# One core, two transformer-like blocks: the first input tile loaded ahead of the constants, gate loads in four buffers, and the last products of a feed-forward layer in another order

## The reference, cut to what matters

```python
def first_block(x, ...):
    h = rms_norm(x, norm_mix_g[l])                    # x * rsqrt(mean(x*x) + eps) * g
    proj = h @ w_in[l]
    mla_cols, rw_cols, gate_cols = _split(proj, [MLA_COLS, RWKV_COLS, GATE_COLS])
    o_a = mla_branch(mla_cols, ...)                   # attention, 8 heads
    o_b = rwkv7_branch(rw_cols, ...)                  # a scan forward and one backward, norm, bonus, gate
    y_a = o_a @ w_o_l[:MLA_WIDTH]
    y_b = o_b @ w_o_l[MLA_WIDTH:]
    gates = jax.nn.sigmoid(gate_cols.reshape(B, S, N_BRANCHES, D) + b_gate[l])
    x = x + (gates[:, :, 0] * y_a + gates[:, :, 1] * y_b) @ w_merge[l]
    h = rms_norm(x, norm_ffn_g[l])
    gp = dwconv_centered(h @ w_ffn_gate[l], ffn_conv_w[l], ffn_conv_b[l])
    x = x + (jax.nn.silu(gp) * (h @ w_ffn_up[l])) @ w_ffn_down[l]
    return x

def second_block(x, ...):
    h = rmsnorm(x, norm1_g[l])
    ...                                               # gated linear attention and a convolution
    x = x + mixed
    h2 = rmsnorm(x, norm2_g[l])
    x = x + (jax.nn.silu(h2 @ w_ffn_gate[l]) * (h2 @ w_ffn_up[l])) @ w_ffn_down[l]
    return rmsnorm(x, norm_f_g)
```

## Time and profile before

| | |
|---|---|
| median of three runs | 3564.58 us (3561.55 to 3566.70) |
| the profiled execution, its own time | 3568.21 us |
| its span in the profile | 3566.4 us |
| PE busy | 3411.8 us, 96% |
| DVE busy | 1707.6 us, 48% |
| ACT busy | 1107.4 us, 31% |
| DMA | 269.82 MB, mean 76 GB/s |

### The profile page before, as it was taken

How to read it: one execution, slowest core, us unless ns; L and a number is a source line. 1 busy time by engine, 2 the same in 40 slices (tenths; PEclk the granted TensorE clock), 3 DMA queues, 4 the chain that set the end, 5 groups by cost and what they waited for, 6 DMA issues and landing times.

```text
span 3566.4 us, 60997 instructions
## 1 busy us (share of the span) xinstructions
PE 3411.8 (96%) x27176; PEld 2715.3 (76%) x27176; DVE 1707.6 (48%) x2528; ACT 1107.4 (31%) x1797; POOL 323.9 (9%) x342
## 2 busy tenths in 40 slices
PE   8989999999999998999999999899899999999998
PEld 7678776777777884578888888687677788888877
DVE  4353555666565566553345433542454522352236
ACT  4323324444444330132224212432332311241124
POOL 1232241111111212000000000001000000000000
PEclk9999999999999999999999999999899999999999
DMA  3241252111111304421112211222003111121122
GB/s 138 68 146 48 77 190 89 59 42 48 58 59 47 100 10 157 145 77 48 48 53 95 71 48 54 95 103 96 24 30 107 65 53 48 59 95 59 48 66 106
DMA packets 89974, 269.82 MB, mean 76 GB/s; under 512 B 11552, under 2 KB 12080, under 8 KB 89712
## 3 DMA queue, kind: packets, MB, share of 16 engines
q1 hardware_dynamic: 78960, 230.26, 19.6%
q0 software_dynamic: 10752, 35.66, 2.9%
HBM read 219.73 MB, written 46.14 MB: 75 GB/s over the span
## 4 chain that ended last, share of the span: by engine, by line
PE 85%; DVE 9%; ACT 3%; issue 2%; DMA 1%; POOL 0%; SPq 0%; DVEq 0%; ACTq 0%; POOLq 0%
PE ps L355 80%; PE ps L354 3%; PE ps L358 2%; DVE SM L375 2%; DVE AR L364 1%; DVE X L364 1%; ACT HT L1144 1%; DVE HT L368 1%; DVE W L364 1%; ACT WS L361 0%; DVE HL L364 0%; ACT W L2056 0%; DVE EX L364 0%; DMA qk_d<-AR 0%; DVE OTB L364 0%
## 5 line engine op out<-in xcount | busy, mean ns | idle before, releaser
L355 PE MATMUL ps<-HH,WS 128*128 128x512 f32 (+1 forms) x3232 | 1001.9, 391 | 0.0
L355 PEld LDWEIGHTS ps<-HH,WS 128*128 128x128 f32 (+1 forms) x3232 | 608.1, 188 | 129.9
L355 PE MATMUL ps<-HL,WS 128*128 128x512 f32 x1616 | 639.9, 396 | 7.1 <-DVE HL L364 6.9
L364 DVE TENSOR_TENSOR WS<-W,WS 128x1024 fp32r<-128x1024 f32 x244 | 298.4, 1223 | 638.2 <-ACT WS L361 638.2
L361 ACT ACTIVATE WS<-W 128x1024 fp32r<-128x1024 f32 x244 | 256.6, 1052 | 892.6 <-PE ps L355 885.4
L355 PE MATMUL ps<-WS,SA 128*128 128x512 f32 x2112 | 491.5, 395 | 23.3 <-DVE SA L364 21.0
L355 PEld LDWEIGHTS ps<-WS,SA 128*128 128x128 f32 x2112 | 401.3, 191 | 110.8 <-issue 27.2
L355 PEld LDWEIGHTS ps<-HL,WS 128*128 128x128 f32 x1616 | 304.1, 188 | 72.9 <-issue 7.4
L355 PE MATMUL ps<-HL,HI 128*128 128x512 f32 (+1 forms) x512 | 208.7, 408 | 4.3 <-POOL WL L364 2.8
L355 PE MATMUL ps<-AR 64*64 64x64 f32 (+2 forms) x4928 | 202.3, 241 | 10.0 <-ACT AR L361 4.2
L355 PE MATMUL ps<-WS,HH 128*128 128x512 f32 x640 | 204.4, 396 | 7.1 <-DVE HL L364 5.4
(11 more groups left out here) (287 smaller groups left out, 4434.4 us busy)
## 6 DMA issues: line engine op xcount, KB each, us to landing
W<-in_w_fd SPq DMA_DIRECT2D x88, 512.0 KB, 3.3
AR<-rw_d SPq DMA_DIRECT2D x104, 256.0 KB, 4.0
W<-in_w_fg SPq DMA_DIRECT2D x44, 512.0 KB, 3.3
W<-in_w_fu SPq DMA_DIRECT2D x44, 512.0 KB, 3.3
W<-in_w_tok SPq DMA_DIRECT2D x24, 512.0 KB, 3.4
rw_d<-X POOLq DMA_DIRECT2D x40, 256.0 KB, 3.4
X<-in_x SPq DMA_DIRECT2D x16, 512.0 KB, 9.0
W<-in_w_g SPq DMA_DIRECT2D x16, 512.0 KB, 3.7
```

Source lines behind the costliest of these rows:

```text
L355: return pe.e.matmul(o, l, r, start=start, stop=stop)
L364: return e.e.tensor_tensor(o, x, y, op)
```

## The change

It has three parts.

- In `first_loads` tile 0 of `x` is issued ahead of `CS` and `PC`. DVE sets one column to 1 and ACT takes its square root before anything else, and DVE and ACT no longer wait for the constants before `rows(0)` and the first `Square`.
- `outa_sp` loads four `WO` and four `GT` when attention is over and stays four ahead. `by_turns` puts four pieces of `outa` in the first turn, and the loader's steps on SP are shifted to match.
- In the last weight tile of the last group of the second part of `down` (in both layers) PE finishes row tiles `j` 0 and 1 for both `kk` before it takes up `j` 2 and 3. A `bk.step()` is put between the adds of `j` 1 and `j` 2.

```diff
         def first_loads(sp):
-            sp.e.dma_start(CS, a["cst"]).then_inc(*dma("dma_cst", "c"))
-            sp.e.dma_start(PC, a["pcols"]).then_inc(*dma("dma_cst", "all"))
             for t in range(NT):
                 sp.e.dma_start(xt(t), a["x"][t * P:(t + 1) * P, :]).then_inc(*dma(f"dma_x{t}", "first"))
+                if t == 0:
+                    sp.e.dma_start(CS, a["cst"]).then_inc(*dma("dma_cst", "c"))
+                    sp.e.dma_start(PC, a["pcols"]).then_inc(*dma("dma_cst", "all"))
...
         def norm1_ve(ve):
-            ve.wait_ge(*at("dma_cst", "all"))
+            ve.e.memset(sm(8, 1), 1.0).then_inc(*ve.sig("ve_norm1", "one"))
...
             rows(0)
+            ve.wait_ge(*at("dma_cst", "all"))
             for t in range(NT):
...
         def norm1_ae(ae):
-            ae.wait_ge(*at("dma_cst", "all"))
+            ae.wait_ge(*at("ve_norm1", "one"))
+            ae.e.activation(sm(8, 1), sm(8, 1), ACT.Sqrt).then_inc(*ae.sig("ae_norm1", "table"))
+
...
-            for n in range(3):
+            for n in range(4):
                 load(n)
-            for i in range(3):
+            for i in range(4):
                 gate(i)
             yield
             for n in range(8):
-                if n + 3 < 8:
-                    load(n + 3)
+                if n + 4 < 8:
+                    load(n + 4)
                 for h in range(2):
-                    if 2 * n + h + 3 < 16:
-                        gate(2 * n + h + 3)
+                    if 2 * n + h + 4 < 16:
+                        gate(2 * n + h + 4)
                     yield
...
-                for _ in range(2 if n else 3):
+                for _ in range(2 if n else 4):
                     next(outa, None)
...
-                        for kk in range(2):
+                        last = f0 and tg and nh and q == nf // 2 - 1
+                        for kk, js_ in ((0, (0, 1)), (1, (0, 1)), (0, (2, 3)), (1, (2, 3))) if last else ((0, range(4)), (1, range(4))):
...
-                            for j in range(4):
+                            for j in js_:
...
-                            bk.step()
+                            if kk or not last:
+                                bk.step()
                     for j in range(4):
                         evac(tg * 4 + j, nh)
+                        if f0 and tg and nh and j == 1:
+                            bk.step()
...
                     evac(tg * 4 + j, nh)
                     if g < 3 and j == 1:
                         part(*divmod(g + 1, 2), 1)
+                    if g == 3 and nf == 10 and j == 1:
+                        bk.step()
...
-            next(outa)
             for n in range(8):
                 next(gn)
                 if n >= 2:
-                    for _ in range(2 if n > 2 else 3):
+                    for _ in range(2 if n > 2 else 4):
                         next(outa)
```

## The result

The changed kernel took 3558.35 us (median of 13 runs, 3548.75 to 3564.21), the kernel before beside it 3564.74 (13 runs, 3560.39 to 3569.22): ratio 0.9981, 95% interval 0.9973 to 0.9990. The forecast was 3558.7, within 0.2% of the kernel before being the likeliest outcome; the result lies at 0.19%, on the edge of it. In two later measurements the changed kernel stood at 0.9978 and 0.9983, so that the three together say 7.4 us (differences of the medians 6.4, 8.8 and 7.0), not 5.9.

What follows compares the result with a forecast made beforehand. PE, busy for 96% of the span, was taken as the bound. −1.8 − 3.43 − 0.3 − 0.5 + 0.3 − 0.2 = −5.9 us against the median 3564.58 gave 3558.7 us, range 3554.0 to 3562.5.

Steps and rivals of the forecast that it cites:

- start: Start of the kernel: earlier first tile and one table load fewer gain 1.8 us, until the load of `w_mla` comes last.
- piece moved: First and last turn: one piece of `outa` moves from the last turn into PE's 7 us idle time, −3.43 us.
- loads no longer in front: First turn: fourth `WO` and `GT` no longer precede the scan outputs, so the first `acc` comes sooner, −0.3 us.
- clock behind the gap: First transposes: PE's gap shrinks from 7.0 to 3.3 us; the clock's fall costs 2.0 instead of 2.5, −0.5 us.
- last products, layer one: Last weight tile of layer one's last group: PE waits for the odd half of `SA`, +0.3 us.
- last products, layer two: End of layer two: PE waits 0.3 us for `SA`, but the first scaling follows the last add at once, −0.2 us.
- the clock holds: Rival, first transposes: the shorter gap keeps 2.4 GHz; 7.6 us gained in all, 3557.0 us; chance 0.22.
- the rise of the clock: Start: PE's longer pause between tiles could shift the rise up to 1.5 us either way, at a price of 0.7.
- the second `acc`: First turn: four adds on DVE make it ready at 1381.95; up to 0.3 us of PE waiting at full clock.
- that rival: First turn: DVE's four adds and later `acc` replace the idle time with a wait; 3559.7 with 1 us beyond; chance 0.06.
- the rival that start and end give nothing: Start and both layers' ends: `w_mla` lands a microsecond later, `SA` waits eat the order's gain; −4.4, 3560.2 us; chance 0.12.
- The rival slower than before: Gaps of about 3 us: the clock falls longer, up to 8.7 us lost, 3567.4 at its bad end; chance 0.06.

Runs made afterwards that it cites:

- the loader alone: Kernel before with the loader four ahead and the first turn still of three pieces: 3564.76 us beside 3566.94, ratio 0.9996.
- five pieces: Changed kernel with five pieces on PE in the first turn and one fewer in the last: 3557.23 us beside 3566.48, ratio 0.9974 to before.

## Why the prediction was right, and where its terms were off

| term | on record | measured |
|---|---|---|
| start | −1.8 (1.0 to 2.4) | −2.2 |
| piece moved | −3.43 | −3.47 |
| loads no longer in front | −0.3 (0 to 0.9) | −0.6 |
| clock behind the gap | −0.5 (−2.5 to +0.9) | −1.55 in the mean |
| last products, layer one | +0.3 | +0.4 |
| last products, layer two | −0.2 | −0.15 |
| sum | −5.9 | −7.6 |

The sum of what the profiles show, −7.6, stands beside −7.4 from three medians. The median of the first measurement, 6.4 under before, lay near the forecast partly by its scatter. That *the clock holds* was priced at 7.6 too is a coincidence: it took the whole 2.5 of the clock and a start of 1.8, where the clock gave 1.55 and the start 2.2. All bounds held.

**Start: the mechanism was right, the size was off.** What was off is the reading of one trace: `w_mla` to land 7.5 us after its issue, at 9.6. It landed 6.7 to 6.8 us after it, at 8.8 to 9.0, in each profile of part one. Without part one, with the same bytes ahead of it, it took 7.5, 7.3, 7.3 and, in the loader alone, 6.8, so the old order can give the early landing too; the trace of before had the latest of the four, and the latest rounding (11.47, against 10.82 in the loader alone). The price set for the rise of the clock, 0.7 either way, was right in size, if the spacing of the products is the clock's: 24 of them took 6.20 to 7.51. How much of the gain each of the two edits of the start gives, no run separates. An estimate from the rows: with the tile first, but both table loads left on ACT's path, the rounding could begin at 4.48 + (11.47 − 7.61) = 8.3, ahead of the landing at 8.87. So the tile's place alone would give all of it, and one table load less only what `w_mla` leaves room for.

**Turns: the piece and the second `acc` as forecast.** No wait of PE stands at the second transposes in any profile with four or five pieces, so that rival is out. The gap was forecast at 3.3; the six are 2.16 to 3.39, mean 2.8. The loads' term, mis-sized by half (0.3 for 0.6), had the right bounds.

**The clock: the term that was mis-sized.** The prediction took nine falls in ten gaps of such length elsewhere in the kernel as the chance here, and 2.0 us as their price. The chance was three in six, the price 1.7: 0.89 in the mean. It took before's cost as 2.5; four profiles with the long gap give 2.36, 3.01, 2.93 and 1.44, mean 2.44. So the gain was 1.55, not 0.5. Why the other gaps fall oftener is open: what PE did before them differs, and no run separated it. The Trainium skill (TensorE: Matmul & The Clock Gate, "HAM oscillation — how this bites in real kernels") lays the fall of the clock to PE's gaps and advises work that keeps PE warm. The measurements side with it only in part: halving the gap kept the clock in half of the profiles, and with no gap it held in all three. Of the rivals, *the clock holds* is thus half true.

**Last products: right, and near nothing.** In layer two the gain at the tail (0.6) and the wait for `SA` (0.44) were both larger than forecast (0.5 and 0.3), with nearly the same difference. In layer one it costs 0.4 and buys nothing. With the start at −2.2, the rival that start and end give nothing is out.

**The rival slower than before** rested on the scatter of the clock, and the scatter is real (3.1 us at one place of layer one), and it comes about between executions of the same kernel. Whether it is as likely with the change as without was not shown: from PE's gap near 1600 us to the end of the span it is 1961.7 us in the mean of the nine profiles with four or five pieces first and 1960.4 in the four others, with a standard deviation of 2 to 3. The medians, 7.4 where the terms add up to 7.6, leave little room for such a price. That the first pair of traces showed 9.6 us less span, and not 7.5, is scatter too.

## What to carry to other kernels

Where one engine is the chain almost throughout, count only work that goes into its idle time: one piece of 3.4 us moved into a 7 us gap gave half of all the gain, and it could be sized to 1% from the timeline. Where a load ends last, see how much waits behind it: taking the first tile ahead of the constants, with the table loads off the path, gave 2.2 us, and the next load ahead only 1.0 more, because another load was then last. And don't read single differences of a few us off one pair of profiles: take the distances between fixed points of the program from several.

## What the runs showed of the hardware that had not been expected

- Behind a gap of the same length the granted clock falls or holds by execution: 3.29 us in one place of layer one, with 3.01 or 4.58 us for the twelve matmuls behind it; behind 2.2 to 3.4 us in the turns, three of six.
- Whole executions of one kernel lie up to 15 us apart, and the clock goes with them: 3548.75 with a mean granted clock of 0.988, 3564.21 with 0.983.
- At the start the 416-column products are spaced 0.35 us at first and 0.19 later, a ratio of 1.8 and so near that of the two levels, while the granted clock reads 1.00 throughout; what slows them is not shown. The place of the change moves by more than 1 us between executions.
- The same 832 KB, with the same bytes ahead of them, landed 6.7 to 6.8 us after their issue in all six profiles with the first tile of `x` ahead of the constants, and 6.8, 7.3, 7.3 and 7.5 us after it in the four with the constants first.
